# A 31-tap depthwise convolution and an attention value product as narrow column products on TensorE (Trainium2, one core)

## The reference, cut to what matters

```python
p = h @ w_in[l]                                   # 384 query latents, 256 key/value latents, 32 rope, 2 x 512 gated
...
sc = einsum("bqhd,bkhd->bhqk", qn, k_nope) + einsum("bqhr,bkr->bhqk", qr, k_rope)
pr = softmax(sc * scale, axis=-1)                 # 8 heads, 512 x 512 each, no mask
y_attn = einsum("bhqk,bkhd->bqhd", pr, v)         # 64 value columns for each head
a, gt = split(p[..., o3:], 2, axis=-1)
u = a * sigmoid(gt)                               # 512 channels
u = dwconv(u, w_dw_conv[l]) + b                   # 31 taps along the tokens, each channel by itself
u = silu(layernorm(u))
x = x + concatenate([y_attn, u]) @ w_o[l]
x = x + ffn(x)                                    # the larger part of a layer's time, not touched
```

## Time and profile before

| | |
|---|---|
| median of three runs | 2043.75 us (2043.48 to 2044.87) |
| profiled execution | 2043.99 us |
| its span, first to last instruction | 2042.3 us |
| TensorE busy | 1952.7 us (96%) |
| VectorE, ScalarE, GpSimd busy | 1195.6, 958.1, 147.2 us |
| mean granted TensorE clock | 0.988 of full |

### The profile page before, as it was taken

One profiled execution on the slowest core, in us unless ns is written; L12 is line 12 of the kernel. 1 busy time (PEld: TensorE's weight loads), 2 busy tenths in 40 slices (PEclk: granted clock), 3 DMA queues, 4 the chain that ended last, 5 costly groups with the idle time before them and its releaser, 6 DMA issues.

```text
span 2042.3 us, 25795 instructions
## 1 busy us (share of the span) xinstructions
PE 1952.7 (96%) x8419; PEld 1540.2 (75%) x8419; DVE 1195.6 (59%) x1960; ACT 958.1 (47%) x1722; POOL 147.2 (7%) x148
## 2 busy tenths in 40 slices
PE   8999989799999988999999999999999999999997
PEld 6777778578888866765678888887766578888886
DVE  4555446643343346888566666436698757656534
ACT  4655563343443333477553444334377554434432
POOL 2111000100000003220010000003120010000000
PEclk9999989899999999999999999999999999999998
DMA  4222213133332222221123333333221033333322
GB/s 136 62 64 68 70 54 104 42 94 96 98 98 94 96 78 63 62 37 37 47 83 103 98 89 106 95 96 88 67 43 42 22 95 92 92 103 93 102 94 82
DMA packets 163423, 162.44 MB, mean 80 GB/s; under 512 B 46840, under 2 KB 121550, under 8 KB 163340
## 3 DMA queue, kind: packets, MB, share of 16 engines
q1 hardware_dynamic: 163236, 161.36, 27.1%
q10 hardware_dynamic: 104, 0.03, 0.0%
HBM read 159.24 MB, written 2.10 MB: 79 GB/s over the span
## 4 chain that ended last, share of the span: by engine, by line
PE 88%; DVE 6%; ACT 3%; issue 1%; POOL 1%; DMA 0%; SPq 0%; DVEq 0%; ACTq 0%; POOLq 0%
PE bank_b L2062 15%; PE bank_b L2064 15%; PE bank_b L2063 15%; PE bank_a L2062 12%; PE bank_a L2064 12%; PE bank_a L2063 12%; PE bank_b L2353 3%; PE bank_b L2451 2%; PE bank_a L2164 1%; PE bank_a L2437 1%; DVE x_t L1338 1%; DVE arena L1341 1%; DVE w_lo L1338 1%; DVE arena L1338 1%; DVE h_lo L1341 1%
## 5 line engine op out<-in xcount | busy, mean ns | idle before, releaser
L1338 DVE TENSOR_TENSOR w_lo<-w_raw,w_hi 128x512 fp32r<-128x512 f32 (+3 forms) x621 | 428.3, 702 | 611.0 <-ACT w_hi L1053 365.4
L1053 ACT ACTIVATE w_hi<-w_raw 128x512 fp32r<-128x512 f32 (+3 forms) x396 | 233.0, 599 | 441.9 <-PE bank_b L2064 227.8
L2062 PE MATMUL bank_b<-h_hi,w_hi 128*128 128x512 f32 x944 | 371.2, 393 | 7.4 <-DVE var L1356 3.9
L2063 PE MATMUL bank_b<-h_lo,w_hi 128*128 128x512 f32 x944 | 367.9, 390 | 0.0
L2064 PE MATMUL bank_b<-h_hi,w_lo 128*128 128x512 f32 x944 | 367.8, 390 | 0.0
L2062 PE MATMUL bank_a<-h_hi,w_hi 128*128 128x512 f32 x592 | 235.2, 397 | 30.8 <-DVE h_lo L1341 16.3
L771 ACT ACTIVATE w_hi<-w_raw 128x512 fp32r<-128x512 f32 x225 | 137.8, 629 | 259.4 <-PE bank_b L2064 138.5
L1341 DVE SCALAR_TENSOR_TENSOR arena<-arena,cols_all 128x512 f32<-128x512 f32 x350 | 244.9, 750 | 0.1
L2063 PE MATMUL bank_a<-h_lo,w_hi 128*128 128x512 f32 x592 | 233.1, 394 | 0.0
L2064 PE MATMUL bank_a<-h_hi,w_lo 128*128 128x512 f32 x592 | 233.0, 394 | 0.0
L2062 PEld LDWEIGHTS bank_b<-h_hi,w_hi 128*128 128x128 f32 x944 | 177.5, 188 | 49.0 <-issue 5.0
(11 more groups left out here) (262 smaller groups left out, 2495.9 us busy)
## 6 DMA issues: line engine op xcount, KB each, us to landing
w_raw<-in_w_up_dram SPq DMA_DIRECT2D x240, 256.0 KB, 3.0
w_raw<-in_w_down_dram SPq DMA_DIRECT2D x152, 256.0 KB, 2.5
w_raw<-in_w_in_dram SPq DMA_DIRECT2D x64, 128.0 KB, 2.3
w_raw<-in_w_gate_dram SPq DMA_DIRECT2D x32, 256.0 KB, 2.9
w_raw<-in_w_in_dram SPq DMA_DIRECT2D x32, 256.0 KB, 2.6
w_raw<-in_w_o_dram SPq DMA_DIRECT2D x32, 256.0 KB, 2.6
w_raw<-in_w_out_dram SPq DMA_DIRECT2D x16, 256.0 KB, 2.6
w_raw<-in_w_in_dram SPq DMA_DIRECT2D x16, 192.0 KB, 2.3
```

The costliest lines, as they stand in the source:

```text
L1053: nc.scalar.activation(w_hi[:, s, 0:c], w_raw[:, s, 0:c], ACT.Copy).then_inc(w_round, 1)
L1338: return nc.vector.tensor_tensor(out_, a, b, op)
L2062: nc.tensor.matmul(out_, a_hi, b_hi, start=start, stop=False, skip_group_check=loose)
L2063: nc.tensor.matmul(out_, a_hi, b_lo, start=False, stop=False, skip_group_check=loose)
```

## The change: what it does, and its diff

The convolution is taken wholly off VectorE. The padded input of a channel tile is copied by 16 transfers, issued by ScalarE, into a stack: for each group `c` of 32 channels a tile whose 128 partitions hold those 32 channels four times, each copy shifted by one more token. A product with a 128x32 weight matrix (four taps of 32 channels) then adds four taps, into 32 partitions of the PSUM bank. A tile takes eight groups of taps times four products. The stacks take two places, so tiles 2 and 3 wait until the products of tiles 0 and 1 have read theirs. `base` now adds the bias for every tile and gives `conv_ready` itself. Tile 0's products move from the `M_KV` chunks to behind the fifth `M_Q` chunk.

The loop takes the two heads of a pair in turns, block by block. A value product becomes eight products of 64 weight columns and 128 queries, for the two heads in turns, each into its half of the partitions; the zero columns and their memset go. The scaling of the probabilities moves from ScalarE to VectorE, right behind the reciprocal. The tap weights come by eight small transfers for each layer in place of one, at the kernel's start.

```diff
-PE_TAPS = 8
-DVE_TAPS = CONV_K - PE_TAPS
+SHIFTS = 4
+GROUPS = -(-CONV_K // SHIFTS)
+LANES = P // SHIFTS
+STACK = S + SHIFTS * (GROUPS - 1)
-EXP_LAG, TURN_LAG, PV_LAG = 2, 4, 8
+EXP_LAG, TURN_LAG, PV_LAG = 2, 4, 6
...
@@ block.sync: tap weights
-                sp_.dma_start(rows_tap[n], w_dw_conv[n]).then_inc(rows2_land, 16)
+                for g in range(GROUPS):
+                    k0, k1 = g * SHIFTS, min(g * SHIFTS + SHIFTS, CONV_K)
...
@@ block.gpsimd
+                        taps = cols_all[:, l, c:c + SHIFTS].unsqueeze(2).broadcast_to((P, SHIFTS, LANES))
+                        nc.gpsimd.tensor_tensor(diag[:, r, :].rearrange("p (c m) -> p c m", c=SHIFTS), taps,
+                                                lanes[:, :].unsqueeze(1).broadcast_to((P, SHIFTS, LANES)),
                                                 ALU.mult).then_inc(diag_made, 1)
-                nc.gpsimd.memset(vv[:, :, :, ND:3 * ND], 0.0).then_inc(vv_zero, 1)
@@ block.scalar
+                def stack_up(j):
+                    act.wait_ge(pad_zero, was[pad_zero.name] + 2)
+                    act.wait_ge(u_ready, was[u_ready.name] + (1, HT, HT, HT)[j])
+                    if j >= 2:
+                        act.wait_ge(diag_used, was[diag_used.name] + (j - 1) * GROUPS)
+                    for c in range(4):
+                        for s in range(SHIFTS):
+                            act.dma_start(stacks[j % 2][s * LANES:s * LANES + LANES, c, :],
+                                          upad[c * LANES:c * LANES + LANES, j, s:s + STACK]).then_inc(stack_land[j % 2], 16)
-                for k in range(4, KT):
+                for k in range(4, 6):
                     split2(M_KV + k)
-                split2(M_Q)
-                act.wait_ge(diag_used, was[diag_used.name] + PE_TAPS)
-                nc.scalar.activation(conv_odd[1], conv_banks[0], ACT.Copy).then_inc(conv_base, 1)
-                for k in range(1, 4):
+                stack_up(0)
+                for k in range(6, KT):
+                    split2(M_KV + k)
+                stack_up(1)
+                for k in range(4):
                     split2(M_Q + k)
...
                 split2(M_PAIR + 1)
+                base(0)
+                stack_up(2)
                 act.wait_ge(sq_added, added0 + KT - 1 + KVT - 1)
                 for t in range(QT):
                     act.wait_ge(lat_ready, was[lat_ready.name] + KVT + t + 1)
                     square(bank_b[:, t, :], ...)
...
@@ block.scalar, attention loop
-                        act.wait_ge(p_step, was[p_step.name] + n + 1)
-                        nc.scalar.activation(prob[:, b, :], prob[:, b, :], ACT.Copy,
-                                             scale=soft[:, 3, b:b + 1]).then_inc(p_ready, 1)
                     if g == 0:
                         base(1)
+                        stack_up(3)
                         copy_key(1, 0)
-                    if m == 0 and i >= 2:
-                        round_out(i - 2)
+                    if m == 6 and i >= 1:
+                        round_out(i - 1)
@@ block.vector: every call of taps() goes
                         nc.vector.reciprocal(soft[:, 3, b:b + 1], soft[:, 2, b:b + 1]).then_inc(p_step, 1)
+                        dve.wait_ge(p_step, was[p_step.name] + n + 1)
+                        nc.vector.tensor_scalar(prob[:, b, :], prob[:, b, :], soft[:, 3, b:b + 1], None,
+                                                ALU.mult).then_inc(p_ready, 1)
@@ block.tensor
-                        nc.tensor.matmul(conv_banks[j], diag[:, r, :], upad[:, j, DVE_TAPS + r:DVE_TAPS + r + S],
-                                         start=r == 0, stop=r == PE_TAPS - 1).then_inc(diag_used, 1)
+                        for c in range(4):
+                            rows = slice(c * LANES, c * LANES + LANES)
+                            last = nc.tensor.matmul(conv_banks[j][rows, :], diag[:, r, rows],
+                                                    stacks[j % 2][:, c, SHIFTS * r:SHIFTS * r + S],
+                                                    start=r == 0, stop=r == GROUPS - 1)
+                        last.then_inc(diag_used, 1)
...
-                pe.wait_ge(conv_base, was[conv_base.name] + 1)
+                pe.wait_ge(conv_ready, was[conv_ready.name] + 1)
                 total(bank_b[:, 3, :], added0 + KT - 1 + KVT - 1 + QT - 1)
...
-                    i, hd, b = g // (2 * TT), g // TT % 2, g % TT
+                    i, b, hd = g // (2 * TT), g // 2 % TT, g % 2
...
-                    part = nc.tensor.matmul(bank_b[:, i % 2, :], vv[:, kb, i, hd * P:hd * P + P], pts[hd][:, kb, :],
-                                            start=hd == 0 and kb == 0, stop=hd == 1 and kb == TT - 1)
+                    for kb in range(TT):
+                        for hd in range(2):
+                            rows = slice(hd * ND, hd * ND + ND)
+                            last = nc.tensor.matmul(bank_b[rows, i % 2, c], vv[:, kb, i, rows],
+                                                    pts[(2 * j + hd) % len(pts)][:, kb * P:kb * P + P],
+                                                    start=kb == 0, stop=kb == TT - 1)
```

More of the change, by code:

```diff
@@ L331, in two_blocks @@
         lat_hi, lat_lo = split[:, 0:5, :], split[:, 5:10, :]
-        pts = (arena[:, 0:4, :], sq[:, :, :])
+        pts = [arena[:, n, :] for n in range(4)] + [sq[:, n, :] for n in range(4)]
         kq_hi, kq_lo = ([[h[:, 2 * q + hd, :] for hd in range(2)] for q in range(2)] for h in (h_hi, h_lo))
@@ L675, in _ @@
                                          base=-P, pattern=[[1, 2 * P]], channel_multiplier=-1))
+            for c in range(P // LANES - 1):
+                made(nc.gpsimd.tensor_tensor(lanes[:, :], (lanes if c else ident)[:, 0:LANES],
+                                             ident[:, (c + 1) * LANES:(c + 2) * LANES], ALU.add))
             def add_squares(count, before_sq, before_add, before_stat):
@@ L1428, in first_normed @@
                                         ALU.mult).then_inc(xn_first, 1)
+            for rows in rows_tap:
+                nc.vector.memset(rows[P - LANES:P, P - LANES:P], 0.0).then_inc(tap_zero, 1)
             dve.wait_ge(cols_made, 1)
@@ L1810, in _ @@
                 for k in range(6, KT):
                     split2_lo(M_KV + k)
-                    taps(2)
-                split2_lo(M_Q)
-                taps(10)
-                for k in range(1, 4):
+                for k in range(4):
                     split2_lo(M_Q + k)
-                    taps(1)
                 dve.wait_ge(w_used, was[w_used.name] + M_KV + KT)
@@ L1830, in _, with rstd_after @@
                 nc.vector.tensor_copy(rot[second, 0, :], rot[first, 0, :]).then_inc(kr_step, 1)
-                def rstd_after(number, bank, width, beside):
+                def rstd_after(number, bank, width, beside=None):
                     dve.wait_ge(stat_ready, number)
@@ L1837, in rstd_after @@
                     stt(var[:, :], bank, 1.0 / width, epsv, ALU.mult, ALU.add).then_inc(var_ready, 1)
-                    beside()
+                    if beside is not None:
+                        beside()
                     dve.wait_ge(guess_ready, number)
@@ L1934, in _ @@
                             split2_lo(M_PAIR + (i + 2) * SLOTS + (2, 4, 5, 6).index(m))
-                    if m == 1 and 2 <= i:
-                        dve.wait_ge(o_round, was[o_round.name] + i - 1)
-                        rest(o2_lo[:, i - 2, :], bank_b[:, i % 2, :], o2_hi[:, i - 2, :]).then_inc(o_split, 1)
-                    taps(taps_by(g, first_taps) - tap)
+                    if m == 7 and 1 <= i:
+                        dve.wait_ge(o_round, was[o_round.name] + i)
+                        rest(o2_lo[:, i - 1, :], bank_b[:, (i - 1) % 2, :], o2_hi[:, i - 1, :]).then_inc(o_split, 1)
                 dve.wait_ge(o_round, was[o_round.name] + HT)
@@ L2363, in _ @@
                     last.then_inc(w_used, 1)
-                    if k == 4:
-                        pe.wait_ge(proj_out, was[proj_out.name] + 8)
-                        conv_taps(0, range(PE_TAPS))
+                pe.wait_ge(proj_out, was[proj_out.name] + 8)
                 for k in range(KT):
```

165 lines of the change are left out of this document (60 added, 105 removed).

## The result

The changed kernel takes 2086.31 us (median of four runs, 2084.13 to 2088.66), the kernel before in the same session 2043.62 us: ratio 1.0208, 95% interval 1.0191 to 1.0226. It is slower by 42.7 us. The profiled execution has a span of 2082.4 us against 2042.3.

A forecast was written before the change was run, and what follows sets the result against it. TensorE, busy 96% of the span, was taken as the bound; the terms sum to +28.3 us a layer, +56.6 for two layers on 2044.0, so 2100 us. Range 2078 to 2125 for the mechanism, 2020 to 2130 overall (0.8).

The forecast's parts named there:

- The prediction's own sign of being wrong: Convolution on TensorE: under 30 us a layer, or ScalarE issues under 0.1 us each, would show the forecast wrong.
- The new products: Convolution on TensorE: quarters overlap but starts keep program order, so a group of four takes 1.82 us; +30.7 us a layer.
- rival A: Convolution: quarters overlap fully, a group of four costs one product, 0.86 us; 2039 us in all; chance 0.37.
- the first rule cited in the prediction: TensorE: products in different column groups start about 4 ns apart, factor 2.38 measured for three of 32 columns.
- ScalarE's transfers: Stack transfers in ScalarE's list: sixteen issues take 5.1 us (ends 1 and 8), delaying splits and squares; +8.1 us a layer.
- Value products: Attention loop on TensorE: 128 products in two overlapping halves, 0.135 us each, 17.3 in place of 27.5 us; -10.2 a layer.
- Changes of shape: TensorE, where products of another array shape begin and end: some 52 changes of 0.09 us; +4.7 us a layer.
- Relief: Attention loop: with scaling off ScalarE and taps off VectorE, TensorE's 5.8 us of waits mostly go; -5.0 us a layer.
- the expected sign: Attention loop: TensorE's wait for the scaled probabilities, now on VectorE, is below 1 us.
- The prediction's narrower range for its own mechanism: Whole kernel: 2078 to 2125 us, from weight loads at none or all and sixteen issues at 1 or 8 us.
- Rival B: Convolution: quarters do not overlap at all, a group takes 3.44 us; +91.1 us a layer, 2226 us; chance 0.13.
- Rival C: Attention loop: quarters overlap fully, but the softmax chain holds the loop, value products give nothing; 2066 us; 0.07 with the rest.

The follow-up runs named there:

- experiment 1: Changed kernel with tiles 0 and 1 writing all eight tap groups of one array quarter in a row, then the next quarter's: 2150.77 us, ratio 1.0536.
- experiment 2: Changed kernel with tiles 0 and 1 writing two products in a row for each array quarter: 2086.31 us in a single run.
- experiment 3: Changed kernel stacking only channels 0 to 31 of each tile, four transfers in place of 16, read by all quarters (other channels' convolution left out): 2025.43 us.
- experiment 5: Changed kernel with padded input written once to DRAM and four reads a stack, issued by ScalarE at other places, 17 issues a layer, not 64: 2026.12 us.
- experiment 7: experiment 5 with the change's own 16 on-chip transfers a stack in place of four reads from DRAM: 2076.87 us, ratio 1.0171.
- experiment 8: experiment 5 with each stack brought by 16 reads of 32 rows from the DRAM copy in place of four: 2055.76 us, ratio 1.0066.
- experiment 11: experiment 5 with the scaling of the probabilities back on ScalarE: 2037.53 us, ratio 0.9971.
- experiment 10: Kernel before with only value products in halves and heads in turns; scaling stays on ScalarE, convolution as before: 2040.75 us, ratio 0.9992.
- experiment 4: Changed kernel with padded input written once a layer to DRAM and each stack read back by four transfers, all issued by SyncE: 2035.05 us, ratio 0.9965.

## Why the prediction came out as it did

The time lies in the predicted range and on the predicted side, 14 us below the forecast, but its largest term was wrong: two large errors of opposite sign nearly cancel, and that the time agrees is luck. The prediction's own sign of being wrong, "a convolution that takes TensorE under 30 us a layer", came true: it takes 28.9.

**The new products: the step failed.** The sentence that failed is "If the four quarters of the array are free of one another but the order holds, the second pass of quarter 0 waits for its first, and the first pass of quarter 1 can start beside it and no sooner." The group was put at 1.82 us and measured 0.88 (a tile 7.0 us in place of 14.6); the term was +30.7 us a layer and measured +1.4. Experiments 1 and 2 show what takes its place: the order of starts in the earlier trace rows was seen on products that all used the same columns, and says nothing of products on different ones. A pass waits for the passes on its own quarter, and up to four of these do not keep the next quarter back. I generalised an order that was seen on one set of columns only. This is the mechanism of rival A. By the first rule cited in the prediction, of the Trainium skill's "TensorE: Matmul & The Clock Gate", Part 3, the trace agrees for two-pass float32 (four starts within 0.02 us); with the strict order that the same section states it does not (in experiment 2 the second quarter starts within 0.02 us of the first, ahead of three passes written before it).

**ScalarE's transfers: the mechanism was right, the size wrong by three.** The step put sixteen issues at 5.1 us from the 0.32 us of a single load by SyncE and the cost at +8.1 us a layer. The issue took 0.64 us, 10.2 us a stack, beyond the upper bound of 8. By place, from the waits after less those of before: column sum 9.1 - 1.0 = +8.1 (forecast 5.8), splits of weights 12.7 - 3.7 = +9.0 (forecast 2.3), the keys of the second pair behind stack 3 +6.7 (forecast 0, or 3.3 with fast groups). Together +23.8. Experiments 3, 5, 7 and 8 show that it is these issues: their number, and the longer issue of the on-chip source. The issue time alone explains the miss: with 10.2 in place of 5.1 and fast groups, the prediction's own steps give 12.5 for the splits, 10.9 for the column sum and 8.4 for stack 3, 31.8 in all, which is more than was measured. For stack 3 the cover had been counted in groups of 1.82 us that were half as long.

**A term that was not in the sum.** In the three longest gaps TensorE's clock drops to one half, and some 6.7 us a layer are lost behind them. Before, there was no such gap in this stage, but the trace of before has them in the first block, and the price could have been read there:

```profile
390.98 0.76 PE L2062 MATMUL bank_a<-h_hi,w_hi 128*128 128x512 f32 x1 [8.18 <-DVE h_lo L1341]
391.54 0.63 PE L2063 MATMUL bank_a<-h_lo,w_hi 128*128 128x512 f32 x1
```

Ten records behind this gap start 0.43 us or more apart in place of 0.23, some 2 us lost behind a gap of 8.2.

**Value products: right.** 1.02 to 1.09 us for eight products of two blocks, forecast 1.1; the term -10.2 measured -11.2. **Changes of shape:** +4.7 forecast; the price of one change comes out (PE's starts beside a convolution piece are 0.32 us apart from 893.07 to 893.39 and 0.33 from 900.40 to 900.73, in place of 0.23), but the balance leaves only 2.2 for all of them and everything unnamed, and their sum was not measured by itself.

**Relief: too large for the changed kernel.** Of the 5.8 us that TensorE waited for the scaled probabilities 4.5 remain (seven waits for `L1894`), so the forecast's -5.0 measured -1.3, and the expected sign, a wait below 1 us, did not come. The move itself is worth 5.7 us a layer (experiment 11), but much of that replaces waits that the shorter value products and the new order of heads bring (experiment 10: 10.2 us). All seven waits that remain lie between 962 and 999 us, behind the last convolution products of the loop (954 us): there TensorE has too little else in its list to cover a block's way through maximum, exponential and scaling, however free VectorE is.

**Put together, per layer:** forecast +30.7 - 10.2 + 4.7 + 8.1 - 5.0 = +28.3. Measured +1.4 - 11.2 + 2.2 + 23.8 + 6.7 - 1.3 = +21.6, and the other waits -0.8 (before, a short one for the exponential), which is the 20.8 of the balance. The prediction's narrower range for its own mechanism, 2078 to 2125, is not what its ends add up to: -6 and -8, +9 and +8 us a layer give 2072 to 2134, and 2140 when the convolution's loads in full (+3) are added as well. Rival A had the products right, and with issues of 8 us for sixteen gave 2058; what it lacked is the last 2 us a stack and the clock. Rival B fell. Rival C was not what held this kernel, but its idea shows in experiment 10, where the shorter value products give nothing: the waits of the loop grow, above all the one for ScalarE's scaling, and the clock falls with them.

## What to carry to other kernels

A transfer issued by ScalarE is work on that engine: count the issues, at 0.47 us (source in DRAM) or 0.64 us (on-chip source) each, and look for one transfer with more rows in place of many small ones, even by way of DRAM (four issues in place of sixteen were worth 30 us of this kernel, the source in DRAM 21 more). Float32 products on the four 32-column quarters of the array overlap fully if neighbours in the list use different quarters; interleave them by ones or pairs, not by eights. And check the granted clock behind an idle time of several microseconds on TensorE: where it fell, the products behind it cost some 2 us more (6.7 us a layer for three gaps).

## What was not expected of the hardware

- Two-pass float32 products of 128x32 on four column quarters: 0.88 us for four, as for one of 128x128 (0.86), when written in turns or in pairs; 22.5 us for the 64 records when written eight in a row for a quarter, where only the last four passes of a quarter overlap with the next.
- An issue on ScalarE's queue: 0.47 us with a source in DRAM at 32 and at 128 partitions alike, 0.64 us with an on-chip source, and mostly 0.32 and 0.52 us for the first of a stack. Why the source matters stays open.
- The clock does not follow the length of a gap alone: it stayed at 1.00 behind a wait of 3.78 us in the changed kernel, and fell among waits of at most 1.7 us in experiment 10's loop.
- Between the issue of experiment 4's write and that of its first read, which waits for the write to land, lie 4.8 us (828.72 to 833.53). SyncE fills 1.5 of them with two weight loads and stands still for the rest. In experiment 5 ScalarE has three weight splits between the two, and the wait does not show.
